# Adding the causal mask of the first attention on VectorE, to a table of key blocks, instead of by a matmul

## The chip, the cores and the metric

The kernel runs on one core of one Trainium2 chip. The metric is the device time of one launch, in microseconds, as the median of three runs. Each launch computes two transformer blocks, one after the other, for one sequence of 512 tokens of width 1024, in fp32. Large products are done in "fp32r" halves: each fp32 operand is split into a rounded high part and a low remainder, and a product takes three matmuls (high by high, high by low, low by high).

## What is computed

The change touches one piece of the first block, the forgetting attention (`fox`). Per head, with causal order and blocks of 128 queries:

```python
def fox_branch(qb, kb, vb, log_f):
    c = jnp.cumsum(log_f, axis=1)               # (B, S, 8 heads)
    c_k = jnp.transpose(c, (0, 2, 1))
    def block(args):
        causal = key_pos[None, :] <= q_pos[:, None]
        logits = jnp.einsum('bqhd,bshd->bhqs', q_blk, kb) * scale
        logits = logits + jnp.transpose(cq_blk, (0, 2, 1))[..., None] - c_k[:, :, None, :]
        logits = jnp.where(causal[None, None], logits, NEG)
        probs = jax.nn.softmax(logits, axis=-1)
        return jnp.einsum('bhqs,bshd->bqhd', probs, vb)
```

The term of the query, `cq`, is the same for a whole row of the softmax and drops out of it. What has to be added to the scores is therefore the key's term, -8 c_k (before the scale of 1/8), and a very large negative number for keys after the query. The second attention of this block (`dsa`), its two in the second block (`swa`, `mla`), the gates, the projections and the feed-forward layer are not changed.

## The kernel before

All engines run their own instruction lists and meet at semaphores. TensorE (PE) does the products; ScalarE (ACT) rounds weights to their high part, copies banks out and takes exponentials; GpSimd (POOL) makes most low parts of the weights and scales probability rows; VectorE (DVE) does the rest; SyncE's queue (SPq) issues every DMA.

The `fox` attention has 8 heads of 4 query blocks, so 32 tiles i = 4h + b. Tile (h, b) has 128 queries and b + 1 key blocks of 128. `attention("fox")` (lines 1742 to 1793) is PE's loop over i. In step i it

1. waits, where b = 0, for the head's operands `fQ`, `fK` (semaphore `head_landed`, line 1750), then computes the scores of tile i into one of two PSUM banks: two matmuls (line 1756), and a third one, in bf16, of a 128x128 identity with a 128x128 mask (line 1758), which adds the mask to the tile's last key block;
2. does a step of "side" work (line 1692, products of the gate and query projections, three matmuls a step in most steps);
3. transposes the probabilities of tile i - 4 (line 1770), and
4. in two steps out of four multiplies a head's probabilities with the values (line 1788).

`softmax` (lines 1196 to 1246) is DVE's loop over the same i: it waits for the scores, then one instruction (line 1214, shown as CUSTOM_DVE_ANT_0) adds the key bias and takes the row maximum, and frees the bank; then come the reciprocal of the row sum of tile i - 2 (1224), the bias of the exponential (1231), and the low part of the transposed probabilities of tile i - 5 (1236). In some steps there is more: the high parts of two heads' queries and keys (`split_pair`, 1260, at i = 6 and 14), the output of a head (1204), and a gate tile (1136). DVE works strictly in this order. Its first loop step comes after `low_half` (1280), the low part of a weight chunk.

The key bias of a head is a row of 512 numbers that every partition needs. `cT` (8 heads x 512) is written once to DRAM (`cum_scratch`, line 620); `load_cum(h)` (588) reads row h back to all 128 partitions of buffer `cB[h % 2]`, 256 KB. SPq issues heads 0 and 1 early. For h = 2 to 7 (lines 627 to 631) it waits until line 1214 has freed the last score tile of head h - 2, issues `load_cum(h)`, and then the six DMAs of `stack_head(h)` (599 and 600, 128 KB each), which copy the head's high and low parts on top of each other into `fQ` and `fK`. PE's wait at the start of head h is for these six.

The mask's two bf16 tables, `diag16` and `ident16`, are made by two DVE casts at lines 1340 and 1341, early in the kernel.

Of the kernel before, what the change touches and what calls it, by code (L numbers as in the profile page):

```python
# [19 lines left out]
F32 = mybir.dt.float32  # L20
F32R = mybir.dt.float32r
BF16 = mybir.dt.bfloat16
ALU = mybir.AluOpType
ACT = mybir.ActivationFunctionType

P = 128
S = 512
NB = S // P
# [3 lines left out]
H = 8  # L32
# [193 lines left out]


PAIR_HI_AT, PAIR_LO_AT = {6: 2, 14: 3}, {6: 2, 14: 3}
ROUNDS_KA, ROUNDS_PAIR, ROUNDS_VB, ROUNDS_NEXT = 2, 7, 1, 1
# [69 lines left out]
def build(nc, dram, out):  # L299
    ctx = ExitStack()  # L300
    with ctx:
        def sb(name, shape, dt=F32):
            return ctx.enter_context(nc.sbuf_tensor(name, shape, dt))
# [13 lines left out]
        ident = sb("ident", [P, P])  # L317
        ident16 = sb("ident16", [P, P], BF16)
        diag16 = sb("diag16", [P, P], BF16)
        ones = sb("ones", [P, P])  # L320
# [47 lines left out]
        pT = place("pT", 44, [P, 2, PT_W, P], F32R)  # L368
        cB = place("cB", 98, [P, 2, S])

# [72 lines left out]
        gains_landed, cst_landed, small_landed, p_landed = sem("gains_landed"), sem("cst_landed"), sem("small_landed"), sem("p_landed")  # L443
        ones_ready, half_ready = sem("ones_ready"), sem("half_ready")
        sq_ready, sum_ready, rt_ready = sem("sq_ready"), sem("sum_ready"), sem("rt_ready")
# [33 lines left out]
        x_dram = nc.dram_tensor("x_scratch", (P, KD * S), F32, kind="Internal").ap()  # L479
        cum_dram = nc.dram_tensor("cum_scratch", (H, S), F32, kind="Internal").ap()  # L480

# [91 lines left out]
        def _(sp_):  # L573
# [14 lines left out]
            def load_cum(h):  # L588
                sp_.dma_start(cB[:, h % 2, :], cum_dram[h:h + 1, :].broadcast_to([P, S])).then_inc(cum_landed[h % 2], 16)

# [21 lines left out]
            for c in range(2, len(CHUNKS)):  # L612
# [4 lines left out]
                if c == UNITS["vb"][0]:  # L617

                    wait_emptied(sp_, "cum", 0)
                    sp_.dma_start(cum_dram, cT[:, :]).then_inc(cum_stored, 16)  # L620
                    sp_.wait_ge(cum_stored, 16)
                    for h in range(2):
                        load_cum(h)
# [497 lines left out]
        def _(dve):  # L1121
# [74 lines left out]
            def softmax(name, sc_, pt, k_bias, rows, att):  # L1196
# [3 lines left out]
                for i in range(NU + LAG_PV + 2):  # L1200
# [6 lines left out]
                    if 0 <= i < NU:  # L1207
                        h, b = a.units[i]
                        k0, k1 = a.keys(b)
                        n = (k1 - k0) * P  # L1210
                        if i >= RING:
                            wait_filled(dve, name + ".t", i - RING)
                        wait_filled(dve, name + ".l", i)
                        empties(dve.tensor_tensor_reduce(  # L1214
                            out=sc_[:, i % RING, 0:n], in0=bank_of(name + ".l", i)[:, 0:n], in1=k_bias(h, b),
                            scale=1.0, scalar=-3e38, op0=ALU.add, op1=ALU.max, accum_out=mx[:, i:i + 1]),
                            name + ".l", i)
# [121 lines left out]
            rms(1)  # L1339
            dve.tensor_copy(ident16[:], ident[:])  # L1340
            dve.tensor_copy(diag16[:], tab("causal")[:, 3 * P:4 * P]).then_inc(half_ready, 1)
            dve.wait_ge(small_landed, 32)
# [62 lines left out]
            dve.wait_ge(qb_scaled, 8)  # L1405
            dve.wait_ge(cum_stored, 16)
            for j in range(2):
                split_pair(j)
            for b in range(NB):
                if b % 2 == 0:  # L1410
# [5 lines left out]
                                                 op0=ALU.mult, op1=ALU.subtract), "vb", b)  # L1416

            def fox_bias(h, b):
                if b == 0:
                    dve.wait_ge(cum_landed[h % 2], 16 * (h // 2 + 1))  # L1420
                return cB[:, h % 2, 0:(b + 1) * P]

            for q in range(2):
                low_half(UNITS["ga"][0] + 1, q)
            softmax("fox", sp, pT, fox_bias, low_rows, attB)
            top_rounds(ROUNDS_NEXT)
# [208 lines left out]
        def _(pe):  # L1635
# [106 lines left out]
            def attention(name, scores, values, sc_, pt, v_stage=None):  # L1742

                a = ATT[name]
                for i in range(NU + LAG_PV + 1):
                    if i < NU:
                        h, b = a.units[i]
                        k0, k1 = a.keys(b)
                        if b == 0 and name == "fox":
                            pe.wait_ge(head_landed[h % 2], 96 * (h // 2 + 1))  # L1750
                        if b == 0 and name == "mla":
                            pe.wait_ge(mla_lo_ready, 2 * h + 2)
                        o = open_bank(name + ".l", i)[:, 0:(k1 - k0) * P]
                        pairs = scores(h, slice(b * P, (b + 1) * P), slice(k0 * P, k1 * P))
                        for m, (q, k) in enumerate(pairs):
                            ins = pe.matmul(o, q, k, start=(m == 0), stop=(m == len(pairs) - 1))  # L1756
                        if name == "fox":
                            ins = pe.matmul(o[:, b * P:(b + 1) * P], ident16[:], diag16[:], start=False, stop=True,
                                            skip_group_check=True)
                        fills(ins, name + ".l", i)  # L1760
# [85 lines left out]
            pe.wait_ge(cst_landed, 32)  # L1846
            pe.wait_ge(half_ready, 1)
            pe.wait_ge(split_lo, NB)
# [208 lines left out]
```

## Time and profile before

| | us |
|---|---|
| median of 3 runs | 1223.14 (1222.91 to 1224.77) |
| the profiled execution, its own time | 1223.25 |
| its span in the trace | 1221.5 |

TensorE is busy 98% of the span. DVE is busy 51%, ScalarE 44%, GpSimd 42%. The clock that TensorE was granted is at its upper level throughout. The `fox` attention, the stage of the change, runs from about 128.5 to about 200 us; its 32 score tiles lie between 128.5 and 179 us. In the rows further down a timeline line gives the start, the duration, engine, line, operation and operands; a bracket gives the idle time before and what ended it. A matmul's duration includes its passage through the array, and matmuls overlap, so what one costs is read from the distance of starts.

### The profile page before, as it was taken

What the parts mean: (1) busy time and instruction counts of PE and PEld (TensorE: products, weight loads), DVE (VectorE), ACT (ScalarE), POOL (GpSimd) and SP (SyncE); (2) the same over time, 40 slices, a digit from 0 to 9 for tenths busy, and PEclk for the clock granted to TensorE, in tenths of its full rate; (3) what the DMA queues carried; (4) which work ended last, traced back from release to release, by engine and by line L of the source; (5) the groups of instructions that cost most, each with busy time, mean ns of one, the idle gap of its engine ahead of it and who ended that gap; (6) DMA issues with size and microseconds to landing.
All of it is one profiled execution on the core that took longest, in us unless ns stands there. A gap on an engine that the chain in (4) does not pass through costs nothing.

```text
span 1221.5 us, 15788 instructions
## 1 busy us (share of the span) xinstructions
PE 1199.2 (98%) x5892; PEld 998.3 (82%) x5892; DVE 627.9 (51%) x1486; ACT 542.0 (44%) x980; POOL 515.6 (42%) x281
## 2 busy tenths in 40 slices
PE   9999999999999999999999999999999999999998
PEld 8878778888888887689878877788888888888886
DVE  5789765784437184984855685845222231220002
ACT  6452673476523354544855476434333222331113
POOL 1428362444443424035353594443443434433441
PEclk9999999999999999999999999999999999999999
DMA  8204652203322523143013212333233332323221
GB/s 272 88 19 148 165 172 72 101 2 103 111 81 84 190 71 103 52 143 119 21 45 98 70 35 84 124 104 104 73 103 101 104 104 77 102 97 121 89 85 69
DMA packets 71419, 119.19 MB, mean 98 GB/s; under 512 B 5672, under 2 KB 33192, under 8 KB 70960
## 3 DMA queue, kind: packets, MB, share of 16 engines
q1 hardware_dynamic: 71344, 118.19, 29.8%
q8 instruction: 47, 0.77, 0.3%
q14 instruction: 28, 0.23, 0.1%
HBM read 107.67 MB, written 4.21 MB: 92 GB/s over the span
## 4 chain that ended last, share of the span: by engine, by line
PE 86%; DVE 6%; ACT 3%; POOL 2%; issue 1%; DMA 1%; SPq 0%; ACTq 0%; DVEq 0%; POOLq 0%
PE bank L1692 65%; PE bank L2024 9%; PE bank L1788 2%; PE bank L1756 2%; PE bank L1770 2%; PE bank L1834 2%; PE bank L1732 2%; DVE sc L1396 2%; DVE m L1392 1%; POOL w_lo L699 1%; POOL w_lo L682 1%; PE bank L1873 1%; ACT w_hi L801 0%; DVE sc L1214 0%; DVE rB L1155 0%
## 5 line engine op out<-in xcount | busy, mean ns | idle before, releaser
L682 POOL TENSOR_TENSOR w_lo<-w_raw,w_hi 128x2048 fp32r<-128x2048 f32 (+4 forms) x82 | 365.1, 4453 | 571.8 <-ACT w_hi L769 518.4
L1692 PE MATMUL bank<-aH,w_hi 128*128 128x512 f32 x800 | 318.8, 398 | 2.3 <-DVE mx L1214 0.9
L1692 PE MATMUL bank<-aH,w_lo 128*128 128x512 f32 x800 | 312.0, 390 | 0.0
L1692 PE MATMUL bank<-aL,w_hi 128*128 128x512 f32 x800 | 308.8, 390 | 0.0
L769 ACT ACTIVATE w_hi<-w_raw 128x2048 fp32r<-128x2048 f32 (+4 forms) x78 | 143.9, 1845 | 262.5 <-PE bank L1692 161.3
L1692 PEld LDWEIGHTS bank<-aL,w_hi 128*128 128x128 f32 x800 | 150.1, 188 | 32.4
L1692 PEld LDWEIGHTS bank<-aH,w_hi 128*128 128x128 f32 x800 | 150.7, 188 | 31.7 <-issue 2.0
L1692 PEld LDWEIGHTS bank<-aH,w_lo 128*128 128x128 f32 x800 | 150.6, 188 | 26.5 <-issue 0.2
L1136 DVE TENSOR_TENSOR fg<-bank,rB 128x512 f32<-128x512 f32 x22 | 15.1, 691 | 128.2 <-PE bank L1692 128.2
L1692 PE MATMUL bank<-w_hi,aH 128*128 128x512 f32 (+4 forms) x224 | 77.1, 344 | 1.1 <-ACT aH L1017 0.7
L1692 PE MATMUL bank<-uH,w_hi 128*128 128x512 f32 x192 | 75.1, 391 | 0.7 <-DVE uL L1588 0.6
L1692 PE MATMUL bank<-w_lo,aH 128*128 128x512 f32 (+4 forms) x224 | 75.4, 337 | 0.0
L1692 PE MATMUL bank<-uL,w_hi 128*128 128x512 f32 x192 | 74.7, 389 | 0.0
L1692 PE MATMUL bank<-uH,w_lo 128*128 128x512 f32 x192 | 74.7, 389 | 0.0
L1692 PE MATMUL bank<-w_hi,aL 128*128 128x512 f32 (+4 forms) x224 | 72.0, 337 | 0.0
L2024 PE MATMUL bank<-w_hi,fH 128*128 128x512 f32 x176 | 68.6, 390 | 0.0
L2024 PE MATMUL bank<-w_hi,fL 128*128 128x512 f32 x176 | 68.5, 389 | 0.0
L2024 PE MATMUL bank<-w_lo,fH 128*128 128x512 f32 x176 | 68.5, 389 | 0.0
L836 ACT ACTIVATE pT<-bank 128x256 fp32r<-128x256 f32 (+3 forms) x128 | 52.7, 412 | 30.8 <-PE bank L1770 29.6
L1236 DVE TENSOR_TENSOR pT<-bank,pT 128x256 fp32r<-128x256 f32 (+3 forms) x128 | 58.3, 457 | 12.4 <-ACT pT L836 12.4
L1624 DVE TENSOR_SCALAR qs<-qs 128x1 f32<-128x1 f32 x4 | 0.6, 154 | 113.4 <-ACT sq L1108 113.4
L713 POOL TENSOR_SCALAR sp<-sp,rsum 128x128 f32<-128x128 f32 (+1 forms) x64 | 34.0, 533 | 51.7 <-DVE rsum L1224 51.6
(324 smaller groups left out, 2133.1 us busy)
## 6 DMA issues: line engine op xcount, KB each, us to landing
w_raw<-in_w_in SPq DMA_DIRECT2D x23, 1024.0 KB, 5.0
w_raw<-in_w_gate SPq DMA_DIRECT2D x22, 512.0 KB, 3.8
w_raw<-in_w_up SPq DMA_DIRECT2D x22, 512.0 KB, 4.7
w_raw<-in_w_down SPq DMA_DIRECT2D x11, 1024.0 KB, 4.8
w_raw<-in_w_merge SPq DMA_DIRECT2D x8, 1024.0 KB, 4.9
w_raw<-in_w_out SPq DMA_DIRECT2D x8, 1024.0 KB, 5.0
w_raw<-in_w_ple_gate SPq DMA_DIRECT2D x4, 1024.0 KB, 5.0
w_raw<-in_w_in SPq DMA_DIRECT2D x4, 512.0 KB, 7.7
```

What stands on the lines that cost most here:

```text
L682: pool.tensor_tensor(out=w_lo[:, c % 2, 0:n], in0=w_raw[:, c % 2, 0:n], in1=w_hi[:, c % 2, 0:n].bitcast(F32), op=ALU.subtract).then_inc(w_ ...
L713: pool.tensor_scalar(s, s, rsum[:, i:i + 1], 1.0, ALU.mult, ALU.mult).then_inc(scaled, 1)
L769: act.activation(w_hi[:, c % 2, 0:n], w_raw[:, c % 2, 0:n], ACT.Copy).then_inc(w_hi_ready, 1)
L836: act.activation(p_views(a, u, pt, 0), t_view(a, u), ACT.Copy).then_inc(p_hi, 1)
L1236: empties(dve.tensor_tensor(out=p_views(a, u, pt, 1), in0=t_view(a, u), in1=p_views(a, u, pt, 0).bitcast(F32), op=ALU.subtract), name + ". ...
L1396: ins = dve.match_replace(out=sc[:, lo:hi], in_to_replace=m8[:, b - 1, :], in_values=sc[:, lo:hi], imm_value=TAKEN)
L1692: ins = pe.matmul(o, l, r, start=(kk == 0 and operand == ROUNDED and m == 0), stop=(kk == total - 1 and operand == REST), skip_group_check ...
L1732: ins = pe.transpose(o[0:rows, b * P:(b + 1) * P], src(b), ident[:])
L1756: ins = pe.matmul(o, q, k, start=(m == 0), stop=(m == len(pairs) - 1))
L1770: ins = pe.transpose(o[:, at * P:(at + 1) * P], src, ident[:])
L1788: ins = pe.matmul(o[:, cols], values(h, kb).rearrange("p c d -> p (c d)"), probs, start=(kb == 0 and part_ == 0), stop=(kb == 2 and part_ ...
L2024: ins = pe.matmul(bank_of("down", i)[:], l[:, kk, tok], r[:, k, col], start=False, stop=(kk == NF - 1 and m == 2), skip_group_check=True)
```

## The change

The third matmul of each score tile is gone, with its two bf16 tables and the two casts that make them. The mask is added to the key bias instead, before the bias is used, by DVE.

For that the bias of a head becomes a table of eight key blocks of 128: places 0 and 1 hold key blocks 0 and 1, places 2 to 5 key blocks 0 to 3, place 6 key block 2, place 7 key block 0. It is laid out so in DRAM by four DMAs from `cT` instead of one. `load_cum` now reads 1024 numbers to each partition, 512 KB for a head instead of 256 KB. Two DVE instructions a head add the 128x128 mask to place 1 and to places 5, 6 and 7. Query block 0 then reads place 7; block 1 places 0, 1; block 2 places 0, 3, 6; block 3 places 2 to 5. The masks of head 0 are added before the loop, those of head h + 1 in DVE's step b = 2 of head h, after the wait for that step's scores and ahead of its line 1214; they begin with a wait for that head's table to have landed.

```diff
+BIAS_BLOCKS = ((0, 0, 2), (2, 0, 4), (6, 2, 1), (7, 0, 1))
+BIAS_OF = ((7, 8, 1), (0, 2, 1), (0, 7, 3), (2, 6, 1))
...
-        ident16 = sb("ident16", [P, P], BF16)
-        diag16 = sb("diag16", [P, P], BF16)
+        sb("pad0", [P, P])
...
-        cB = place("cB", 98, [P, 2, S])
+        cB = [place(f"cB{i}", at, [P, 2 * NB, P]) for i, at in enumerate((98, 127))]
...
             def load_cum(h):
-                sp_.dma_start(cB[:, h % 2, :], cum_dram[h:h + 1, :].broadcast_to([P, S])).then_inc(cum_landed[h % 2], 16)
+                row = cum_dram[h:h + 1, :].broadcast_to([P, 2 * S])
+                sp_.dma_start(cB[h % 2][:, :, :].rearrange("p c k -> p (c k)"), row).then_inc(cum_landed[h % 2], 16)
...
                     wait_emptied(sp_, "cum", 0)
-                    sp_.dma_start(cum_dram, cT[:, :]).then_inc(cum_stored, 16)
-                    sp_.wait_ge(cum_stored, 16)
+                    for place_, kb, n in BIAS_BLOCKS:
+                        sp_.dma_start(cum_dram[:, place_ * P:(place_ + n) * P], cT[:, kb * P:(kb + n) * P]).then_inc(cum_stored, 16)
+                    sp_.wait_ge(cum_stored, 16 * len(BIAS_BLOCKS))
...
                         empties(dve.tensor_tensor_reduce(
-                            out=sc_[:, i % RING, 0:n], in0=bank_of(name + ".l", i)[:, 0:n], in1=k_bias(h, b),
+                            out=shaped[0], in0=shaped[1], in1=k_bias(h, b),
...
-            dve.tensor_copy(ident16[:], ident[:])
-            dve.tensor_copy(diag16[:], tab("causal")[:, 3 * P:4 * P]).then_inc(half_ready, 1)
...
+            def mask_bias(h):
+
+                dve.wait_ge(cum_landed[h % 2], 16 * (h // 2 + 1))
+                for a, n in ((1, 1), (5, 3)):
+                    t = cB[h % 2][:, a:a + n, :]
+                    mask = tab("causal")[:, 3 * P:4 * P].rearrange("p (o k) -> p o k", o=1).broadcast_to([P, n, P])
+                    dve.tensor_tensor(out=t, in0=t, in1=mask, op=ALU.add).then_inc(bias_masked, 1)
+
             def fox_bias(h, b):
                 if b == 0:
-                    dve.wait_ge(cum_landed[h % 2], 16 * (h // 2 + 1))
-                return cB[:, h % 2, 0:(b + 1) * P]
+                    dve.wait_ge(bias_masked, 2 * h + 2)
+                if b == 2 and h + 1 < H:
+                    mask_bias(h + 1)
+                first, end, step = BIAS_OF[b]
+                return cB[h % 2][:, first:end:step, :]
...
+            mask_bias(0)
             softmax("fox", sp, pT, fox_bias, low_rows, attB)
...
-                        if name == "fox":
-                            ins = pe.matmul(o[:, b * P:(b + 1) * P], ident16[:], diag16[:], start=False, stop=True,
-                                            skip_group_check=True)
...
-            pe.wait_ge(half_ready, 1)
```

## Rows read from the trace of the kernel before

**Rows 1.** The page: busy time, and the chain that ended last by engine.
```profile
PE 1199.2 (98%) x5892; PEld 998.3 (82%) x5892; DVE 627.9 (51%) x1486; ACT 542.0 (44%) x980; POOL 515.6 (42%) x281
PE 86%; DVE 6%; ACT 3%; POOL 2%; issue 1%; DMA 1%; SPq 0%; ACTq 0%; DVEq 0%; POOLq 0%
```
**Rows 2.** PE's timeline, one tile of `fox` with the mask matmul.
```profile
153.80 0.40 PE L1756 MATMUL bank<-fK,fQ 128*128 128x256 f32 x2
154.04 0.23 PE L1758 MATMUL bank<-diag,ident 128*128 128x128 bf16 x1
...
154.40 0.39 PE L1692 MATMUL bank<-aH,w_lo 128*128 128x512 f32 x1
```
**Rows 3.** PE's timeline, two heads' starts of `dsa`, and its like tile.
```profile
248.02 0.39 PE L1756 MATMUL bank<-kaS,qaS 128*128 128x128 f32 x2
...
249.69 0.40 PE L1756 MATMUL bank<-kaS,qaS 128*128 128x256 f32 x2
...
250.16 0.40 PE L1692 MATMUL bank<-aH,w_lo 128*128 128x512 f32 x1
...
254.45 0.39 PE L1756 MATMUL bank<-kaS,qaS 128*128 128x128 f32 x2
```
**Rows 4.** PE's timeline, the starts of `fox` heads 2 to 5 and 7.
```profile
138.38 0.44 PE L1756 MATMUL bank<-fK,fQ 128*128 128x128 f32 x2 [0.69 <-DMA fK<-kbT]
...
145.10 0.44 PE L1756 MATMUL bank<-fK,fQ 128*128 128x128 f32 x2 [0.20 <-DMA fK<-kbT]
...
152.05 0.39 PE L1756 MATMUL bank<-fK,fQ 128*128 128x128 f32 x2
...
158.94 0.39 PE L1756 MATMUL bank<-fK,fQ 128*128 128x128 f32 x2
...
171.97 0.39 PE L1756 MATMUL bank<-fK,fQ 128*128 128x128 f32 x2
```
**Rows 5.** DVE's timeline, the weight half ahead of the loop and the first maximum.
```profile
126.20 2.35 DVE L1280 TENSOR_TENSOR w_lo<-w_raw,w_hi 128x1024 fp32r<-128x1024 f32 x2
129.02 0.29 DVE L1214 CUSTOM_DVE_ANT_0 sp<-bank,cB 128x128 f32<-128x128 f32 x1 [0.47 <-PE bank L1758]
```
**Rows 6.** DVE's timeline, step b = 2 of head 1, and b = 2 to b = 3 of head 3.
```profile
135.03 0.56 DVE L1214 CUSTOM_DVE_ANT_0 sp<-bank,cB 128x384 f32<-128x384 f32 x1 [0.57 <-PE bank L1758]
...
149.04 0.55 DVE L1214 CUSTOM_DVE_ANT_0 sp<-bank,cB 128x384 f32<-128x384 f32 x1
...
150.03 0.42 DVE L1260 CAST oddQ<-qbT 128x512 fp32r<-128x512 f32 x1
...
150.70 0.68 DVE L1214 CUSTOM_DVE_ANT_0 sp<-bank,cB 128x512 f32<-128x512 f32 x1
```
**Rows 7.** SPq's timeline, loads of heads 2 and 3.
```profile
132.10 0.34 SPq L589 DMA_DIRECT2D cB<-cum_scratch  x1
...
138.02 0.34 SPq L589 DMA_DIRECT2D cB<-cum_scratch  x1
```
**Rows 8.** DMA issues of the page (KB each, median us from issue to landing), and of tile cB alone.
```profile
w_raw<-in_w_gate SPq DMA_DIRECT2D x22, 512.0 KB, 3.8
...
DMA to landing us min/median/max: 3.5/3.5/4.7
```
**Rows 9.** Windows while head 2 is loaded: busy engines, clock, DMA share, GB/s.
```profile
133.00:134.50 1.50, 1.50 (x12) 1.28 (x10) 0.82 (x5) 0.78 (x5) 0.67 (x2) 1.00 0.59 199
134.50:136.00 1.50, 1.50 (x10) 1.17 (x10) 0.96 (x5) 0.87 (x3) 0.68 (x2) 1.00 0.92 260
```
**Rows 10.** DVE adds that read two SBUF tensors, and a broadcast table: timeline.
```profile
30.74 0.76 DVE L1136 TENSOR_TENSOR rp<-tmI,cst 128x256 f32<-128x256 f32 x2
...
205.29 0.42 DVE L1172 TENSOR_TENSOR tmA<-tmA,rp 128x256 f32<-128x256 f32 x1
```
**Rows 11.** The same kind of add beside a GpSimd instruction: DVE's, then POOL's timeline.
```profile
42.78 4.60 DVE L1173 TENSOR_TENSOR sm<-sm,rp 128x32 f32<-128x32 f32 x1
...
42.70 4.63 POOL L682 TENSOR_TENSOR w_lo<-w_raw,w_hi 128x2048 fp32r<-128x2048 f32 x1 [5.62 <-ACT w_hi L769]
```

## What the change does to the time

> **What bounds the kernel now.** I read the page first: TensorE is busy for 98% of the span and the chain that ended last lies on it for 86% [rows 1]. So time taken off TensorE's list is worth its full length, unless something else becomes late. Then I read TensorE's timeline in the stage of the change, between 128.5 and 182 us. TensorE runs without a gap there except at two places: it waits 0.69 us at the start of head 2 and 0.20 us at the start of head 3, both for the operands `fK` that DMAs bring [rows 4]. Those two rows say which supply is closest to being late. The third view is the timelines of DVE and of SPq in the same stage, since the change moves work to the one and doubles a transfer in front of the other.
>
> **What the mask matmul costs.** Its duration is 0.23 us, but matmuls overlap, so I compare like stretches with and without it. In `fox`, tile b = 1, the second side matmul starts 0.60 us after the scores begin (154.40 - 153.80) [rows 2]; in `dsa`, whose tiles have no mask matmul, 0.47 us (250.16 - 249.69) [rows 3]. Over a whole head, from start to start, `fox` takes 6.89 us (158.94 - 152.05) [rows 4] and `dsa` 6.43 us (254.45 - 248.02) [rows 3], with the same matmuls otherwise. The mask costs 0.46 us a head, and 8 heads give **3.7 us** on the path. That is the most that the change can bring. The two casts that go lie on DVE at 30 us, where TensorE waits for nothing; I count them as nothing.
>
> **What the change adds on DVE.** Two adds a head of 128x128 and 128x384, both from SBUF. The nearest row, 128x256, takes 0.42 us, and two of them with a broadcast table take 0.76, so the next one starts after 0.34 and the broadcast costs nothing [rows 10]. At about 0.13 us a block of 128 and 0.07 fixed, the pair occupies 0.2 + 0.5 = 0.70 us.
>
> For head 0 this stands ahead of the loop. The weight half ends at 128.55 and the first maximum starts at 129.02 [rows 5], so it moves to about 129.35: 0.35 us later, and TensorE's third tile waits for that bank. Cost: 0.35 us, once.
>
> For the others it stands in step b = 2, and its wait matters more than its work. Call R(h) the moment at which the last maximum of head h is done; SPq then issues the table of head h + 2 (132.10 for h = 0, 138.02 for h = 1) [rows 7]. The masks of head h + 1, added during head h, wait for the table that was issued at R(h - 1). Before, DVE asked for it nearly a head later. Now DVE reaches the wait for table 2 at 135.03 [rows 6], 2.9 us after its issue, while even the 256 KB table takes 3.5 us to land [rows 8]. So **DVE stands still**, with the maxima of b = 2 and b = 3 queued behind the wait; the latter is R(h), on which the next table hangs. It is a ring: table landed, masks, maximum b = 2, maximum b = 3, release, next table.
>
> **The ring in numbers.** From the start of maximum b = 2 to that of b = 3 head 3 takes 1.66 us, of which 0.67 is the pair of casts at 150.03 [rows 6]; plain it is 0.99. From the start of maximum b = 3 to the release is 0.72 (head 3's last maximum starts at 150.70 and SPq issues the next table at 151.42). Extra DVE work between the two maxima: head 1 both casts and a gate tile, 1.27; heads 2 and 5 a gate tile, 0.61; head 3 the casts, 0.67; head 4 none. Together 3.16 us for heads 1 to 5.
>
> The landing of 512 KB instead of 256 KB is the unknown. From one side: weight loads of 512 KB land in 3.8 us [rows 8], 0.3 more. From the other: while only the table is in flight the windows show about 200 GB/s at a DMA share of 0.59 [rows 9]; 256 KB more at that rate are 1.3 us, and the slowest of the present loads, one of two issued together, took 4.7 [rows 8], 1.2 more. Queueing behind six other DMAs could make it 1.7. I take 0.8, between the weight row and the rate, since the pieces get longer but come from the same single row of DRAM. With 0.05 us from release to issue: 3.5 + 0.8 + 0.05 = 4.35.
>
> So R(h) = R(h - 1) + 4.35 + 0.70 + 0.99 + 0.72 + extra = R(h - 1) + 6.76 + extra. R(0) is 132.05 + 0.35 = 132.4. R(5) = 132.4 + 5 x 6.76 + 3.16 = **169.4**. I checked the other limit on R(h), TensorE's own head start plus about 6.35 us and the extra: it is earlier in each of heads 3 to 5.
>
> **What TensorE sees of it.** Head h starts when its six stacking DMAs have landed, and they are issued behind the table. Before, from release to start, it was 6.3 us for head 2 (138.38 - 132.10) and 7.1 us for head 3 (145.10 - 138.02) [rows 4, 7]. The DMA share is 0.92 as soon as they run [rows 9], so a longer table pushes them back; 0.6 us of the 0.8 I let through, since the first window has room. The bounds are nothing and 1.2. So L = 6.3 + 0.6 = 6.9. Head 7 starts at R(5) + 6.9 = **176.3**, where it started at 171.97 [rows 4]: 4.3 us late. Heads 2 to 6 start late by the same rule, and all the matmul time saved in them is spent waiting. Only head 7's 0.46 us remains. After that TensorE has its work queued again, and the delay goes to the end of the kernel undiminished.
>
> **The sum.** 4.3 - 0.46 = +3.8 us. The profiled execution took 1223.25 us with a span of 1221.5; the median of the runs is 1223.14, 0.1 lower, so it stands for them. **1223.25 + 3.8 = 1227.0.**
>
> The side terms: the three additional small stores at 90 us, about 0.35 us of issue each, and 512 KB more ahead of a weight load delay that load by 2 to 2.5 us. ScalarE takes it 3.4 us after it has landed, so it is hidden; if that cover went, up to 2 us. The maxima read one strided table operand in new shapes; the bank operand and the count of elements are as before, so I put it at nothing, up to 0.1 us each if not.
>
> **A rule beside the rows.** An add of 128x32 from two SBUF operands took 4.60 us, ten times the time of one eight times as large [rows 10], where a GpSimd instruction of 4.63 us had begun 0.08 us before it [rows 11]. It ended with that instruction. The mask adds are of this kind; the maxima, with one operand in PSUM, are not. The Trainium skill, "SBUF — State Buffer", section "SBUF: two separate sides", says it as a rule: the port pair that VectorE and GpSimd share is an exclusive lock, and a VectorE instruction with two SBUF inputs waits out a GpSimd instruction that reads SBUF. By that rule, the trace agrees.
>
> **The rivals.**
>
> *A, the ring* (my forecast). With a table that lands after 3.8 us and L = 6.5 it gives R(5) = 166.7 and about 1224.0; with 5.2 us and L = 7.5, R(5) = 173.5 and 1231.8.
>
> *B, the saving arrives.* The tables land early enough and DVE catches up: 1223.25 - 3.7 + 0.35 = 1219.9. For it: DVE is idle in a quarter of this stage, and in heads 3 to 6 it reaches b = 2 some 4.7 to 5.1 us after the issue. Against it: in head 1 that is 2.9 us, under any landing seen, and each late R(h) makes the next table late too. It decides if tables land within about 3.3 us.
>
> *C, the longer table costs nothing to land.* With 3.55 and 6.3 us the ring takes 5.96 + extra and TensorE's own pace limits half the heads: R(5) = 166.2, head 7 at 172.5, which is 0.55 late, less 0.46: 1223.3, no change.
>
> *D, the shared port.* A, and each of the five masks that count also meets a GpSimd instruction: a row scaling of up to 0.7 us, half of it on average, up to the whole: 2 to 3 us more, 1229.5. Against it: when DVE has waited for a table, GpSimd, fed by DVE's reciprocals, is mostly idle; its 1.3 us instructions fall behind steps that DVE takes after the mask.
>
> That the change does not do what it says, the table in another order, I see no sign of: the blocks written and read agree.
>
> **How the numbers follow.** A 0.68, B 0.08, C 0.12, D 0.12. A change under 0.2%, 2.4 us, can hardly be told from none by a measurement of this kernel; the bounds are 1220.7 and 1225.6. Of A about a fifth lies under 1225.6. Faster: B, 0.08. Same: C and 0.14 of A, 0.26. Slower: the rest of A and D, 0.66. The range leaves out B and the far end of A: 1222.0 to 1231.0.
>
> **What would show it.** Right: no L1758; DVE's longest new idle time before the new adds, ended by the table's DMA, 1 us and more in heads 1 and 2; TensorE waiting at each start of heads 2 to 7 for `fK`; head 7 at about 176. Wrong: TensorE's head period of 6.4 us kept through heads 3 to 7 (B); table landings of 3.5 us (C); mask adds much longer than 0.3 and 0.6 us (D). The forecast fails most easily by the landing time: each 0.1 us there counts five times.

## The result, and the profile after

The changed kernel takes **1230.61 us** (median of 6 runs, 1228.02 to 1231.78), the kernel before beside it 1224.26 us (6 runs, 1222.91 to 1224.77). The ratio is 1.0052, 95% interval 1.0041 to 1.0064: the change costs 6.4 us, and the forecast was 3.8. The 1230.61 lie 0.4 us inside the upper end of the stated range. The profiled execution took 1231.78 us with a span of 1230.0, 8.5 more than the profiled one of before. It is the slowest of its six, 1.2 us above their median (1231.78 - 1230.61), and the profiled one of before is 1.0 us under the median beside it (1224.26 - 1223.25), so what is read from the pair overstates the usual cost by 2.1 us.

The page, its first part (busy time, share, instructions), the chain and the issue of the table:

```profile
PE 1201.7 (98%) x5860; PEld 1001.5 (81%) x5860; DVE 634.4 (52%) x1500; ACT 542.5 (44%) x980; POOL 515.5 (42%) x281
PE 83%; DVE 7%; ACT 3%; POOL 2%; DMA 2%; issue 2%; SPq 1%; DVEq 0%; ACTq 0%; POOLq 0%
cB<-cum_scratch SPq DMA_DIRECT2D x8, 512.0 KB, 4.2
```

TensorE has 32 matmuls fewer than in [rows 1] and is busy for 2.5 us more. The share of DMA in the chain went from 1% to 2%. The waits between 130 and 182 us (total, times, longest) say where:

```profile
DVE cB L1428 <- DMA cB<-cum_scratch: 7.2, 5, 2.3
...
PE bank L1772 <- DMA fK<-kbT: 6.6, 5, 2.5
...
PE bank L1772 <- DVE mx L1220: 1.1, 3, 0.6
```

VectorE waits for the table five times, 7.2 us in all, and TensorE for a head's operands five times, 6.6 us, where [rows 4] had 0.9. The mask adds (L1428) on VectorE's timeline, for heads 2 to 7; the number in brackets is the idle time before them:

```profile
137.03 0.76 DVE L1428 TENSOR_TENSOR cB<-cB,cst 128x128 f32<-128x128 f32 x2 [2.33 <-DMA cB<-cum_scratch]
145.10 0.94 DVE L1428 TENSOR_TENSOR cB<-cB,cst 128x128 f32<-128x128 f32 x2 [2.07 <-DMA cB<-cum_scratch]
152.53 0.76 DVE L1428 TENSOR_TENSOR cB<-cB,cst 128x128 f32<-128x128 f32 x2 [1.18 <-DMA cB<-cum_scratch]
161.82 1.17 DVE L1428 TENSOR_TENSOR cB<-cB,cst 128x128 f32<-128x128 f32 x2
169.56 0.76 DVE L1428 TENSOR_TENSOR cB<-cB,cst 128x128 f32<-128x128 f32 x2 [1.04 <-DMA cB<-cum_scratch]
176.85 1.92 DVE L1428 TENSOR_TENSOR cB<-cB,cst 128x128 f32<-128x128 f32 x2 [0.58 <-DMA cB<-cum_scratch]
```

The chain of work that ended last, followed between 138 and 180 us, walks round the ring once and more. In it one sees a maximum (L1220), the table it releases, the masks, the next two maxima, the release:

```profile
140.06 0.60 DVE sp L1220
140.69 4.29 DMA cB<-cum_scratch
145.00 0.05 DVEq L1424
145.10 0.94 DVE cB L1428 x2
146.04 0.47 DVE sp L1220
...
147.64 0.60 DVE sp L1220
148.27 0.33 SPq L592
...
152.43 4.05 DMA fK<-kbT
156.52 0.46 PE bank L1772 x2
```

The chain of the kernel before crosses a `fK` operand here too, but no table. TensorE's starts of heads 2 to 5 and 7, the answer to [rows 4]:

```profile
139.46 0.47 PE L1772 MATMUL bank<-fK,fQ 128*128 128x128 f32 x2 [1.86 <-DMA fK<-kbT]
147.33 0.44 PE L1772 MATMUL bank<-fK,fQ 128*128 128x128 f32 x2 [0.23 <-DMA fK<-kbT]
156.52 0.46 PE L1772 MATMUL bank<-fK,fQ 128*128 128x128 f32 x2 [2.53 <-DMA fK<-kbT]
164.56 0.39 PE L1772 MATMUL bank<-fK,fQ 128*128 128x128 f32 x2
...
179.57 0.44 PE L1772 MATMUL bank<-fK,fQ 128*128 128x128 f32 x2 [1.31 <-DMA fK<-kbT]
```

Head 7 starts at 179.57, 7.6 us later than before. Its last score tile (the 128x512 of b = 3) starts at 185.31 against 177.50, 7.8 later, so head 7's own 0.46 did not show either. Of the 8.5 us, 7.8 arise before that tile; the last 0.7 lie behind it, and are less than the 1.9 us by which the runs of before differ among themselves.

The windows hold what I had not foreseen (the columns as in [rows 9]: length, five engines, granted clock, DMA share, GB/s):

```profile
139.00:140.00 1.00, 0.54 (x3) 0.54 (x4) 1.00 (x4) 0.68 (x3) 0.00 (x0) 0.87 0.00 0
140.00:143.00 3.00, 3.00 (x9) 2.25 (x9) 3.00 (x16) 1.36 (x5) 1.79 (x3) 0.50 0.42 138
...
156.00:157.00 1.00, 0.48 (x3) 0.48 (x4) 0.22 (x1) 0.60 (x2) 0.21 (x1) 0.90 0.45 61
157.00:160.00 3.00, 3.00 (x11) 2.60 (x12) 1.09 (x5) 0.25 (x1) 2.41 (x3) 0.50 0.99 277
```

After its two longest waits, 1.86 and 2.53 us, TensorE is granted 0.50 of its clock, the lower level of 1.2 GHz, for some 3.5 us. In the 3 us from 140 it does 9 matmuls; the kernel before did 19 in the same 3 us, at a clock of 1.00.

### The profile page after: what moved, and what is told of

Read it like the earlier page. It is cut to its first block, busy times and chain, and to the rows that moved or that the text cites. A ratio compares the mean times of both kernels' runs of the same rounds, so it can differ in the third digit from the quotient of the medians.

```text
span 1230.0 us, 15743 instructions
## 1 busy us (share of the span) xinstructions
PE 1201.7 (98%) x5860; PEld 1001.5 (81%) x5860; DVE 634.4 (52%) x1500; ACT 542.5 (44%) x980; POOL 515.5 (42%) x281
## 4 chain that ended last, share of the span: by engine, by line
PE 83%; DVE 7%; ACT 3%; POOL 2%; DMA 2%; issue 2%; SPq 1%; DVEq 0%; ACTq 0%; POOLq 0%
PE bank L1708 63%; PE bank L2036 9%; PE bank L1801 2%; PE bank L1847 2%; PE bank L1772 2%; PE bank L1748 2%; PE bank L1783 2%; DVE sc L1400 1%; DVE m L1396 1%; POOL w_lo L703 1%; DMA cB<-cum_scratch 1%; POOL w_lo L686 1%; DMA fK<-kbT 1%; PE bank L1885 1%; DVE sp L1220 0%
```

## The experiments

Twelve kernels. A ratio is always to the kernel before, run beside it on the same chip, and differences in us are worked out from the ratios. Those that the argument needs most come first.

**The place of the wait.** The masks of head h + 1 are added at the end of VectorE's step b = 3 of head h, behind the maximum that releases the next table, instead of in step b = 2 ahead of two maxima.

```diff
                 if b == 0:
                     dve.wait_ge(bias_masked, 2 * h + 2)
-                if b == 2 and h + 1 < H:
-                    mask_bias(h + 1)
...
+                    if name == "fox" and i % NB == NB - 1 and i < NU - 1:
+                        mask_bias(i // NB + 1)
```

> The changed kernel, but the masks of head h + 1 are added at the end of DVE's step b = 3 of head h, instead of ahead of the maximum of b = 2. Same adds, same 512 KB table, same three matmuls fewer. Ring theory: DVE no longer stands at the table's transfer with two maxima behind it, the releases come at TensorE's pace, and the time falls to about 1222.5 us (3.7 us of matmuls saved, 0.35 for the first masks, about 2 us left of longer waits at heads 2 and 3). Size theory (the doubled transfer ahead of the six stacking DMAs is the whole loss, wherever the masks stand): still 3 us or more above the kernel before.

Measured: 1225.06 us, ratio 1.0012 (1.0003 to 1.0022), with the same table of 512 KB and the same adds. 4.9 us of the loss are gone (1.0052 less 1.0012). That is 2.6 us more than the ring theory's 1222.5, which counted on the full 3.7 us of saved matmuls, and 1.5 us over the kernel before where the size theory asked for 3 or more. VectorE waits for no table, though the loads take even longer, and TensorE's starts are near those of before:

```profile
139.40 0.44 PE L1772 MATMUL bank<-fK,fQ 128*128 128x128 f32 x2 [1.68 <-DMA fK<-kbT]
...
172.28 0.44 PE L1772 MATMUL bank<-fK,fQ 128*128 128x128 f32 x2 [0.55 <-DMA fK<-kbT]
```

```profile
DMA to landing us min/median/max: 4.0/4.5/5.1
```

(The second fence is the last line of the answer for tile `cB` in the same kernel.) Tables are released at 132.66, 138.24, 144.68, 151.59, 157.66 and 164.68, where the change had 132.72 to 172.55. So the ring is cut with the transfer as long as it was. The edit moves the adds along with their wait, and no run moves the wait by itself; what the adds cost at the early place without a wait is measured below.

**The size of the table.** Only 256 KB are loaded; VectorE makes the other four blocks (a copy and three adds), once at the late place and once where the change has the masks.

```diff
-                row = cum_dram[h:h + 1, :].broadcast_to([P, 2 * S])
+                row = cum_dram[h:h + 1, :].broadcast_to([P, S])
...
+                dve.tensor_copy(t[:, 0, :], t[:, 2, :]).then_inc(bias_masked, 1)
+                for dst, src in ((t[:, 1:8:6, :], t[:, 2:4, :]), (t[:, 6:7, :], t[:, 4:5, :]), (t[:, 5:6, :], t[:, 5:6, :])):
```

> The changed kernel with 256 KB tables: only the four key blocks are loaded, the four others are made on DVE (one block copied, four blocks masked, about 0.9 us a head instead of 0.7), and this is done at the end of step b = 3 as in the run with late masks. Ring and size both gone: it should come to about 0.3 us above the run without any mask (1222.2), so 1222.3 to 1223; what stays of a loss is then DVE's work. Size theory alone: the same. If the late masks still delay the release of the next tables, it stays near 1225.

> The changed kernel with the masks where the change has them (ahead of the maximum of b = 2, with the wait for the table), but with 256 KB tables and the four other blocks made on DVE. Only the landing time in the ring differs (3.5 us instead of 4.2), the masks take 0.9 instead of 0.7 us. Ring theory: six rings of 6.2 us plus the extras instead of 6.9: about 1225.5, half of the loss stays. Size theory: near 1223.

Measured: late 1223.85 us, ratio 1.0001 (0.9991 to 1.0010); early 1229.29, ratio 1.0045 (1.0028 to 1.0062). Both came out above what I expected, the first by 0.9 us, the second by 3.8. In the second the five links from one release to the next sum to 36.8 us (132.98 to 169.77), where rings of 6.2 and the 3.16 of extra work make 34.2. The first of its masking instructions, a copy:

```profile
137.03 0.23 DVE L1424 COPY cB<-cB 128x128 f32<-128x128 f32 x1 [2.27 <-DMA cB<-cum_scratch]
...
144.89 0.23 DVE L1424 COPY cB<-cB 128x128 f32<-128x128 f32 x1 [1.66 <-DMA cB<-cum_scratch]
...
152.12 0.23 DVE L1424 COPY cB<-cB 128x128 f32<-128x128 f32 x1 [0.56 <-DMA cB<-cum_scratch]
```

Even a table of the old size makes VectorE stand for 2.27 us at head 2. This small table landed after 3.2/3.8/5.0 us (min/median/max) against 4.1/4.2/5.2 of the large one. With the two kernels above there is a square, in us over the kernel before:

| | masks behind b = 3 | masks in b = 2 |
|---|---|---|
| table 256 KB | +0.1 | +5.5 |
| table 512 KB | +1.5 | +6.4 |

The place costs 4.9 to 5.4 us, the size 0.9 to 1.4. The intervals of the four entries reach from 1.1 to 2.1 us to either side, so the effect of the place is beyond doubt and that of the size, in this square, is not; the next run shows it by itself.

**The larger table alone.** The kernel before with 512 KB loaded for each head, half of it never read.

```diff
-                sp_.dma_start(cB[:, h % 2, :], cum_dram[h:h + 1, :].broadcast_to([P, S])).then_inc(cum_landed[h % 2], 16)
+                sp_.dma_start(cB[h % 2][:, :], cum_dram[h:h + 1, :].broadcast_to([P, 2 * S])).then_inc(cum_landed[h % 2], 16)
```

> The kernel before with the matmul mask, but each head's key bias is written twice side by side and loaded as 512 KB, of which the second half is never read. Only the size of the transfer changes. Ring theory: the operands of a head land 0.6 us later after a release, which shows at heads 2 and 3 only (0.7 and 0.2 us waits there become about 1.3 each); plus 1 to 2 us in all. Size theory: plus 4 to 6 us.

Measured: 1224.80 us, ratio 1.0013 (1.0004 to 1.0022). The table lands after 4.1/4.4/5.2 us and head 2 waits 1.18 us for its operands instead of 0.69; the other starts move by 0.5 to 0.9, of which 0.4 is there already when head 0 starts (129.00 against 128.58). That is the 1 to 2 us of the ring theory, and not the 4 to 6 of the size theory.

**The adds alone.** The kernel before with the same two adds on spare data in step b = 2, with no wait for a table.

```diff
+                if b == 2 and h + 1 < H:
+                    spare_adds()
```

> The kernel before with its mask matmul and 256 KB tables, and the mask adds of the change at their places on DVE, but on spare data and with no wait for a transfer. It measures DVE's work alone: releases 0.7 us later, which shows at heads 2 and 3 and in heads 6 and 7: plus 1 to 2 us. Ring theory needs it to be clearly less than the change's 6.4 us.

Measured: 1225.94 us, ratio 1.0018 (1.0009 to 1.0027), 2.2 us more than before, a little over what I expected and a third of the change's 6.4. The adds are not free: the pairs take 0.75, 0.76, 0.76, 1.72, 1.17, 0.90, 1.17 and 2.26 us. The longest, on VectorE's timeline, and GpSimd's beside it:

```profile
170.65 2.26 DVE L1424 TENSOR_TENSOR spareB<-sc,cst 128x128 f32<-128x128 f32 x2
172.84 0.54 DVE L1215 CUSTOM_DVE_ANT_0 sp<-bank,cB 128x384 f32<-128x384 f32 x1
```

```profile
170.53 0.70 POOL L714 TENSOR_SCALAR sp<-sp,rsum 128x512 f32<-128x512 f32 x1
171.19 1.32 POOL L700 TENSOR_TENSOR w_lo<-w_raw,w_hi 128x512 fp32r<-128x512 f32 x1
```

The pair spans the rest of the row scaling and the whole weight split, and ends 0.4 us behind the latter (172.91 against 172.51), about as long as the second add takes. The maximum that waits behind it then holds TensorE for 0.97 us at the start of head 7 (173.54).

**The mask matmul alone.** The kernel before without it; the causal mask is left out in the diagonal blocks.

```diff
-                        if name == "fox":
-                            ins = pe.matmul(o[:, b * P:(b + 1) * P], ident16[:], diag16[:], start=False, stop=True,
-                                            skip_group_check=True)
```

> The kernel before without its mask matmul and with nothing in its place: the first attention leaves out the causal mask within the diagonal block. It measures the most that the change can gain. 32 matmuls at 0.115 us: minus 3.7 us if the operands of the heads still land in time; about minus 3.2 if the waits at heads 2 and 3 grow by what was saved ahead of them.

Measured: 1222.19 us, ratio 0.9986 (0.9976 to 0.9996), 1.7 us less where eight heads times 0.46 are 3.7. A head does take 6.44 us (144.04 to 150.48), as reckoned. But head 2 now waits 1.35 us for its operands instead of 0.69, and near the end three engines wait one behind the other (ScalarE, VectorE and TensorE in the same kernel, each line from its own timeline):

```profile
172.93 1.06 ACT L801 ACTIVATE w_hi<-w_raw 128x1024 fp32r<-128x1024 f32 x1 [1.95 <-DMA w_raw<-in_w_in]
174.00 0.60 ACT L830 ACTIVATE low_rows<-bank 64x512 f32<-64x512 f32 x1
...
174.63 0.68 DVE L1204 TENSOR_TENSOR attB<-bank,low_rows 64x512 f32<-64x512 f32 x1 [3.05 <-ACT low_rows L830]
...
175.70 0.73 PE L1756 MATMUL bank<-fK,fQ 128*128 128x512 f32 x2 [0.87 <-DVE mx L1214]
```

**The late weight chunk.** These lines name a suspect: the weights of the following stage, 1 MB, issued behind the operands of head 7. Three kernels load them in two halves, behind the operands of heads 5 and 6 (two of the expectations say 6 and 7; the SyncE timeline shows 5 and 6): the kernel before, the kernel without the mask matmul (the mask left out as above), and the small late table.

```diff
-                load(c)
+                if c != UNITS["qa"][0] + 1:
+                    load(c)
...
                         stack_head(h)
+                        if h in (5, 6):
+                            load_half(UNITS["qa"][0] + 1, h - 5)
```

> The kernel before with one edit: the second weight chunk of the stage that follows first attention is loaded in two halves of 512 KB, behind the operands of heads 6 and 7 instead of whole behind those of head 7. In the kernel before ScalarE waits 1.19 us for these weights at 174.73. Theory (the end of first attention is set by the softmax chain on VectorE, and the weights are hidden beside it): 1223.5, within 0.1% of before. Rival (the wait for the weights is on the path): faster by up to 1.2 us, 1222.4.

> The kernel before without the mask matmul (first attention's causal mask is left out in the diagonal blocks) and with the weight chunk loaded in halves behind the operands of heads 6 and 7. Without the mask matmul alone the time was 0.9986 of before, 1.7 us less, where eight heads times 0.46 make 3.7, and ScalarE waited 1.95 us for this chunk. Theory (the missing 2 us are held by the operands' ring at head 2 and by VectorE's maxima in heads 6 and 7): 1222.0, as without this edit. Rival (the late weight chunk holds them): 1220.3, or 3.3 us less than before.

> The run with small tables and late masks, and the load of the last weight chunk of this stage, which SPq issued behind head 7's operands, is split into halves behind heads 5 and 6. In the run without any mask ScalarE waited 2 us for this chunk in head 7 with the head's output behind it, and TensorE 0.9 us at the end. If that is where half of the saved matmul time went, this gains 1 to 2 us over the run without the split: 1221 to 1222. If the halves only push back the operands of heads 6 and 7, it gains nothing.

Measured: before with it 1223.29 us, ratio 0.9993 (0.9984 to 1.0002); without the mask matmul 1220.65, ratio 0.9973 (0.9962 to 0.9983); small late table 1223.73, ratio 1.0000 (0.9991 to 1.0010). In the second, the rival held: 3.3 us less than before instead of 1.7, and the chain above is gone:

```profile
171.24 1.05 ACT L814 ACTIVATE w_hi<-w_raw 128x1024 fp32r<-128x1024 f32 x1
...
174.97 0.71 PE L1769 MATMUL bank<-fK,fQ 128*128 128x512 f32 x2
```

The last score tile starts 0.73 us before the 175.70 of the kernel without the mask matmul alone, though head 7 starts 0.19 later (169.93 against 169.74). The ratios say 1.6, but their intervals overlap (0.9976 to 0.9996 and 0.9962 to 0.9983), so by the times alone the gain is likely and not shown; that the wait is gone the traces show. As long as the mask is computed somewhere the earlier chunk brings nothing that can be told from none: with the small late table, TensorE waits for VectorE's maxima in head 6 instead (0.49 and 0.57 us, at 168.76 and 170.73).

**The changed kernel with the weights earlier.** First I put the halves in front of the operands of heads 5 and 6 (the expectation says behind; the timeline shows them directly after the table), then behind them.

> The changed kernel with one edit: the second weight chunk of the stage that follows first attention is loaded in two halves, behind the operands of heads 6 and 7. Head 7 starts 7.6 us late in the changed kernel, but its time is 8.5 us over that of the kernel before, and there the chain of waits runs over this chunk, issued at 177.12 and 5.40 us on its way. Theory (the ring of tables costs 7.6 less 0.46 and the late chunk the rest): 0.9 us less than the change, 1.0045 of before, 1229.7. Rival (the chunk is hidden beside the ring): no gain, 1.0052, 1230.6. Second rival (the early halves lie in front of the last table or the last operands and lengthen their landing): slower than the change, 1231.5 or more.

> The changed kernel with the weight chunk loaded in two halves of 512 KB, issued behind the operands of heads 5 and 6. In the run before this one the halves stood in front of those operands: head 5 started 9.8 us after its table's release and the time was 1233.2. Theory (in front they lengthen the ring, behind they don't, and the late chunk costs the changed kernel what head 7's delay does not explain): 0.9 us less than the change, 1.0045 of before, 1229.8. Rival (the late chunk costs nothing beside the ring): as the change, 1.0052, 1230.8. Second rival (behind the operands each half still lies beside the next table and delays its landing): 1231.5 or more.

Measured: in front 1233.18 us, ratio 1.0072 (1.0058 to 1.0086); behind 1230.00, ratio 1.0050 (1.0036 to 1.0064). In front, on SyncE's queue and TensorE's timeline:

```profile
155.83 0.33 SPq L602 DMA_DIRECT2D cB<-cum_scratch  x1
156.26 0.39 SPq L598 DMA_DIRECT2D w_raw<-in_w_in  x1
156.75 0.47 SPq L612 DMA_DIRECT2D fQ<-tQ  x1
```

```profile
165.65 0.45 PE L1785 MATMUL bank<-fK,fQ 128*128 128x128 f32 x2 [3.48 <-DMA fK<-kbT]
```

From release to start head 5 takes 9.8 us, and TensorE stands for 3.48. Heads 2 to 4 of the same kernel take 6.95, 6.95 and 7.43, so half a megabyte ahead of the operands costs 2.4 to 2.9 us there. Behind them the ring is there as in the change (head 7 at 178.34), and the difference of 0.0002 says nothing; whether the late chunk costs the changed kernel anything stays open.

**The clock.** The changed kernel with 7, 10 and 5 spare matmuls ahead of the operand waits of heads 2, 4 and 7, so that TensorE is not idle there.

```diff
+                        if b == 0 and name == "fox" and h in FILL:
+                            spare = open_bank(name + ".l", i)
+                            for _ in range(FILL[h]):
+                                pe.matmul(spare[:], aH[:, 0, 0:P], aH[:, 0, :], start=True, stop=True)
```

> The changed kernel, with 7, 10 and 5 spare 128x512 matmuls (0.23 us each, into the score bank that is written next) ahead of TensorE's waits for the operands of heads 2, 4 and 7, which were idle for 1.9, 2.5 and 1.3 us. If the halved clock after such waits is what took the time beyond my forecast, it stays at its upper level and the time falls by 2 to 3.5 us to about 1227.5, the forecast of the ring without the clock. If the ring sets every head's start by itself and the slow clock hides behind it, the time stays at 1230.5.

Measured: 1229.52 us, ratio 1.0053 (1.0038 to 1.0068), the same as the change. The clock stays up:

```profile
140.00:143.00 3.00, 3.00 (x19) 2.57 (x18) 3.00 (x14) 1.61 (x7) 1.46 (x3) 1.00 0.28 98
156.00:160.00 4.00, 4.00 (x25) 3.45 (x24) 2.55 (x11) 1.88 (x6) 2.51 (x4) 1.00 0.65 178
```

Head 4 now takes 6.52 us from start to start (157.03 to 163.55) instead of 8.04, and the last table is released at 171.06 instead of 172.55. Yet heads 2 and 4 start 0.9 and 0.5 later than in the change, since the filler overruns their operands. At head 7 it does so too:

```profile
177.98 1.46 PE L1769 MATMUL bank<-aH 128*128 128x512 f32 x5 [0.88 <-DVE mx L1221]
179.28 0.34 PE L1777 MATMUL bank<-fK,fQ 128*128 128x128 f32 x2
```

The filler first waits for its score bank and then runs until the head starts. With the change's 7.02 us from release to start, head 7 could have started at 178.1 (an estimate); it starts at 179.28. So the half clock is real, but this run took back with the filler what the clock may have given, and it doesn't decide what the half clock costs.

## Why the prediction came out as it did

**Right: what bounds, and the mechanism.** The ring was to show as VectorE waiting for the table, over 1 us in heads 1 and 2 (measured 2.33 and 2.07), and TensorE waiting for `fK` at each start of heads 2 to 7 (it did at all but head 5). The square bears the mechanism out: with the adds and their wait behind the release, the same adds and the same load cost 1.5 us instead of 6.4, and the adds at the early place without a wait, in a kernel that keeps its mask matmul, cost 2.2. How the difference of 4.9 divides between the wait and the adds ahead of the two maxima no run shows exactly. Rival B needed tables within 3.3 us; the fastest of eight took 4.1. Rival C, a longer table at no cost, fails by the same row; besides, the small table at the early place loses 5.5 us, and its five links sum to 36.8 us where C's ring of 5.96 plus extra makes 32.96.

**Right: the landing.** I took 0.8 us more for 512 KB; the median went from 3.5 to 4.2, 0.7 more. (The bounds given for rival A leave out the 0.05 us from release to issue: by the formula they are R(5) = 166.9 and 1224.2, and 173.9 and 1232.2.)

**The ring, link by link.** From one release to the next, in us, from SyncE's issues of `cB` (132.72, 140.69, 148.27, 155.59, 164.63, 172.55):

| head | 1 | 2 | 3 | 4 | 5 | sum |
|---|---|---|---|---|---|---|
| predicted (6.76 + extra) | 8.03 | 7.37 | 7.43 | 6.76 | 7.37 | 36.96 |
| measured | 7.97 | 7.58 | 7.32 | 9.04 | 7.92 | 39.83 |
| with the clock kept up | 8.16 | 7.61 | 7.76 | 7.60 | 7.08 | 38.21 |
| with the weights behind | 8.08 | 7.58 | 7.58 | 7.72 | 7.57 | 38.53 |

Three of the five measured links are within about 0.2 us. The last row is from a trace of 1229.26 us, 2.5 us shorter than the change's, whose ring is made the same way (releases at 133.00, 141.08, 148.66, 156.24, 163.96 and 171.53). The failed step is head 4, by 2.3 us in the change's trace and by 1.0 in that one, and it is the sentence "I checked the other limit on R(h), TensorE's own head start plus about 6.35 us and the extra: it is earlier in each of heads 3 to 5". In head 4 the table had landed before VectorE came for it (161.82, no wait): VectorE had been waiting for ScalarE's rows of the previous head, 2.17 us until 160.37, and these for TensorE. With the weights behind, too, the table was there first (161.25, no wait). The link of head 4 is then the time from the release of head 3 to the start of head 4 plus the time from there to its own release, and both were longer than I had them:

| head 4 | start after R(3) | start to release | link |
|---|---|---|---|
| predicted | -0.53 | 6.35 | 5.82, so the ring's 6.76 |
| measured | 0.93 | 8.11 | 9.04 |
| with the weights behind | -0.02 | 7.74 | 7.72 |
| with the clock kept up | 0.65 | 6.95 | 7.60 |

The start was late in the change's trace: the operands came 8.25 us after their release (148.27 to 156.52) where I had L = 6.9; SyncE's queue shows two of the six issues held up, one by 0.43 and one of 0.99 long. And head 4 ran at half clock in the first two traces, behind waits of 2.53 and 1.75 us; with the clock kept up it took 6.95. The link has 7.6 to 7.7 us even where the start is in time or the clock is up, so 6.76 was too short in each of the three.

The second miss is in head 5: 7.92 against 7.37. There the table took 4.8 us on the chain (164.63 to 169.47) where I had one landing for all.

**Right: L, for the other heads.** From release to start, 6.74, 6.64, 7.22 and 7.02 us for heads 2, 3, 6 and 7, against 6.9. So head 7 started at 179.57 instead of 176.3 for one reason: R(5) was 172.55 instead of 169.4, 0.3 of it in R(0) and 2.9 in the five links. (The 0.3 in R(0) is there before the ring: VectorE's weight half ahead of the loop starts at 126.47 instead of 126.20. The first masks then add 0.36, as forecast.)

**Wrong by its reason: the 0.46.** I subtracted head 7's mask matmul. By its last score tile three of its four mask matmuls are gone, 0.35 us, but that tile is 7.8 late where the start is 7.6 late. Two distances of starts on TensorE's timeline have grown and make up the difference: from the product with the values (L1801) to the scores of b = 1 it is 1.06 us instead of 0.67, with a wait of 0.22 for a maximum in it, and from the transposes to the scores of b = 3 it is 0.61 instead of 0.46. Of the same kind is "3.7 us on the path. That is the most that the change can bring". The term itself holds (a head takes 6.44 us without it), but 1.7 us came with the matmul alone and 3.3 with the weight chunk earlier as well, which points at supplies that were just in time for the longer head; the two intervals overlap, so this is the likely reading and not a shown one.

**Mis-sized: the adds.** I priced the pair at 0.70. Undisturbed it is 0.75 to 0.76. Rival D, the shared port, was to add 2 to 3 us to the ring. In the changed kernel the six pairs together are 1.8 us longer than undisturbed (6.31 less 6 x 0.76). 0.6 of it lies in the ring, in the pairs of heads 3 and 5, and 1.2 is the pair at 176.85, after the last release. Three of the six are at 0.76: its argument against itself, that GpSimd is mostly idle when VectorE has waited for a table, was right for these. So D is at most a small part of what lifted the result over the forecast. The pair at 176.85 does reach TensorE: the maximum for which head 7 waits 0.22 us comes behind it in VectorE's order. In the kernel with the adds alone, the last five pairs are 3.4 us longer than undisturbed in all. The rule that the Trainium skill gives in "SBUF — State Buffer", section "SBUF: two separate sides", says that such an add waits out a GpSimd instruction that reads SBUF; the pair of 2.26 us beside GpSimd's 0.70 and 1.32 agrees.

**The sum again.** Profiled: +7.8 at head 7's last tile where I had +3.8. Of the 4.0 between, 3.2 are the release R(5) (head 4 alone 2.3), 0.1 is L, and 0.7 the 0.46 that did not come and the 0.2 that head 7 lost on top. The medians put the whole at +6.4: the two profiled executions lie 2.1 us further apart than the medians do. The trace with the weights behind, 6.0 us above the profiled one of before, has the last tile 6.25 late (183.75): there R(5) is 2.1 late (0.6 in R(0), 1.6 in the five links, 1.0 of it head 4), L is 6.81 instead of 6.9, and of the 0.46 only 0.1 arrives. That is the more usual size of the miss, with the caution that this kernel differs from the change in where its weights are loaded. The granted clocks of the change's six runs go from 0.995 (1231.78 and 1231.67 us) to 0.999 (1228.02 us), which fits the half clock making part of the difference between runs; how much stays open.

## What to carry to other kernels

When an operation is moved to an engine with room, ask first what it waits for and what is queued behind it: here the adds cost 2.2 us and the larger load 1.6 when each was alone, while the same adds with their wait cost 4.9 us more ahead of the instruction that releases the next transfer than behind it. A wait belongs behind the release that its own successor depends on, and only then is its size worth tuning. A ceiling of "so many instructions times so long each" asks that every supply that was just in time for the slower engine also comes earlier: of 3.7 us only 1.7 came. Check the waits that are there already; without the mask matmul the 0.69 us at head 2 grew to 1.35 and the 1.19 at the weight chunk to 1.95.

## What the runs showed of the hardware

- TensorE was granted 0.50 of its clock for about 3.5 us (140 to 143 and parts of the us on either side) behind idle times of 1.86 and 2.53 us in the changed kernel, and of 2.24 and 1.75 us in the one with the weights behind. The length of the idle time alone does not decide it: behind waits of 1.68 us (masks late, 139.40), 1.73 (small table early, 139.40) and 2.07 (weights in front, 139.29) the windows that follow are at 1.00. What decides is not shown by these runs.
- One row of DRAM spread to 128 partitions landed after 3.5 us for 256 KB and 4.2 us for 512 KB in the kernels before and after. Over all fourteen kernels the medians are 3.5 to 3.8 us for 256 KB and 4.2 to 4.5 for 512 KB.
- A pair of adds from SBUF of 0.76 us took 1.92 us in the changed kernel and up to 2.26 us in the kernel with the adds alone, beside GpSimd work of 0.70 and 1.28 to 1.32 us.
- Six operand loads issued behind a 512 KB weight load had a head start 9.8 us after the release, against 6.95 to 7.43 at heads 2 to 4 of the same kernel.
